# Odd layer of a fused two-block kernel: projection in 512-column half-contraction chunks, with the attention items issued between its products

## The reference, cut to what matters

```python
def odd_mixer(h, cos, sin, w_in, lam_q1, lam_k1, lam_q2, lam_k2, subln_g, w_out, lambda_init):
    b, s, _ = h.shape
    q, k, v = jnp.split(h @ w_in, 3, axis=-1)
    q = apply_rope(q.reshape(b, s, 2 * N_DIFF_HEADS, DIFF_DIM), cos, sin).reshape(b, s, N_DIFF_HEADS, 2, DIFF_DIM)
    k = apply_rope(k.reshape(b, s, 2 * N_DIFF_HEADS, DIFF_DIM), cos, sin).reshape(b, s, N_DIFF_HEADS, 2, DIFF_DIM)
    v = v.reshape(b, s, N_DIFF_HEADS, 2 * DIFF_DIM)
    lam = (jnp.exp(jnp.sum(lam_q1.astype(F32) * lam_k1.astype(F32)))
           - jnp.exp(jnp.sum(lam_q2.astype(F32) * lam_k2.astype(F32))) + lambda_init)
    o = diff_attention(q, k, v, lam)
    o = rms_norm_2(o, subln_g) * (1.0 - lambda_init)
    return o.reshape(b, s, DIFF_W) @ w_out
...
        s = jnp.einsum('bqhcd,bshcd->bhcqs', qb, k, preferred_element_type=F32) * d ** -0.5
        p = jax.nn.softmax(jnp.where(causal, s, -jnp.inf), axis=-1)
        a = p[:, :, 0] - lam * p[:, :, 1]
        return jnp.einsum('bhqs,bshe->bqhe', a.astype(v.dtype), v)
```

## Time and profile before

| | |
|---|---|
| median of 3 runs | 1993.04 us (1991.38 to 1993.1) |
| profiled execution, its own time | 1991.96 us |
| span of that profile | 1990.3 us |
| mean granted TensorE clock in the span | 0.935 of full |
| projection of the odd layer | 1256.95 to 1398.15 |
| odd layer from there to the start of `mixer_out` | 1398.15 to 1522.22 |

### The profile page before, as it was taken

How to read it: one execution, slowest core, us unless ns; L and a number is a source line. 1 busy time by engine, 2 the same in 40 slices (tenths; PEclk the granted TensorE clock), 3 DMA queues, 4 the chain that set the end, 5 groups by cost and what they waited for, 6 DMA issues and landing times.

```text
span 1990.3 us, 24899 instructions
## 1 busy us (share of the span) xinstructions
PE 1774.3 (89%) x10049; PEld 1484.2 (75%) x10049; DVE 943.5 (47%) x1232; ACT 654.2 (33%) x933; POOL 521.7 (26%) x441
## 2 busy tenths in 40 slices
PE   4997599778697789989999999899677999999997
PEld 3796499568695677668888777799566678888875
DVE  1568577675477764453333222533564343233223
ACT  4312255421223334242322212421564243333113
POOL 0005700344744000358878200078000000000000
PEclk8898799889898889999999999999878999999999
DMA  8453300134522000335556222222100212323321
GB/s 279 156 166 106 106 1 1 66 120 146 180 79 83 1 1 1 127 102 179 194 181 191 92 86 98 65 85 86 42 1 1 85 64 90 100 86 99 101 74 42
DMA packets 154445, 187.22 MB, mean 94 GB/s; under 512 B 6765, under 2 KB 121813, under 8 KB 154356
## 3 DMA queue, kind: packets, MB, share of 16 engines
q1 hardware_dynamic: 154356, 185.96, 29.0%
HBM read 183.85 MB, written 2.10 MB: 93 GB/s over the span
## 4 chain that ended last, share of the span: by engine, by line
PE 61%; POOL 15%; issue 8%; DVE 8%; ACT 5%; DMA 3%; POOLq 0%; SPq 0%; DVEq 0%; ACTq 0%
PE ps L694 7%; PE ps L695 7%; PE ps L696 7%; POOL msum L536 5%; POOL mraw L529 5%; PE ps L712 4%; PE ps L714 4%; PE ps L715 4%; PE ps L1044 4%; PE ps L1045 4%; PE ps L1046 4%; PE ps L788 2%; DMA mfirst<-in_w_mod_dram 1%; DMA mraw<-in_w_mod_dram 1%; PE ps L1017 1%
## 5 line engine op out<-in xcount | busy, mean ns | idle before, releaser
L1044 PE MATMUL ps<-uH,whi 128*128 128x512 f32 x704 | 277.6, 394 | 11.0 <-DVE uL L1581 11.0
L1565 DVE TENSOR_TENSOR wlo<-wraw,whi 128x2048 fp32r<-128x2048 f32 x71 | 176.5, 2487 | 218.8 <-ACT whi L1175 218.6
L1046 PE MATMUL ps<-uH,wlo 128*128 128x512 f32 x704 | 275.6, 392 | 0.0
L1045 PE MATMUL ps<-uL,whi 128*128 128x512 f32 x704 | 275.6, 391 | 0.0
L1175 ACT ACTIVATE whi<-wraw 128x2048 fp32r<-128x2048 f32 x71 | 135.7, 1911 | 346.8 <-PE ps L696 327.9
L712 PE MATMUL ps<-whi,uH 128*128 128x256 f32 (+1 forms) x800 | 230.8, 289 | 11.2 <-DVE uL L1581 11.2
L529 POOL TENSOR_TENSOR mraw<-mraw,cpad 128x1024 f32<-128x1024 f32 x64 | 128.4, 2007 | 398.9 <-PE ps L635 256.6
L714 PE MATMUL ps<-wlo,uH 128*128 128x256 f32 (+1 forms) x800 | 229.4, 287 | 0.0
L715 PE MATMUL ps<-whi,uL 128*128 128x256 f32 (+1 forms) x800 | 229.1, 286 | 0.0
L712 PEld LDWEIGHTS ps<-whi,uH 128*128 128x128 f32 x800 | 157.2, 196 | 12.8 <-issue 12.7
L1044 PEld LDWEIGHTS ps<-uH,whi 128*128 128x128 f32 x704 | 133.2, 189 | 41.1 <-issue 10.8
(11 more groups left out here) (389 smaller groups left out, 3200.6 us busy)
## 6 DMA issues: line engine op xcount, KB each, us to landing
mraw<-in_w_mod_dram SPq DMA_DIRECT2D x104, 512.0 KB, 3.9
wraw<-in_w_gate_dram SPq DMA_DIRECT2D x22, 1024.0 KB, 5.3
wraw<-in_w_up_dram SPq DMA_DIRECT2D x22, 1024.0 KB, 5.5
wraw<-in_w_down_dram SPq DMA_DIRECT2D x16, 1024.0 KB, 5.1
wraw<-in_w_in_odd_dram SPq DMA_DIRECT2D x12, 1024.0 KB, 5.1
wraw<-in_w_in_dram SPq DMA_DIRECT2D x11, 1024.0 KB, 5.4
wraw<-in_w_in_even_dram SPq DMA_DIRECT2D x9, 1024.0 KB, 6.5
mfirst<-in_w_mod_dram SPq DMA_DIRECT2D x16, 512.0 KB, 7.3
```

Of the source, the lines that this page charges most:

```text
L1044: mm(o, h_, uH[:, k], start=(k == 0), stop=False)
L1045: mm(o, h_, uL[:, k], start=False, stop=False)
L1046: last = mm(o, l_, uH[:, k], start=False, stop=(k == KT - 1))
L1565: V.tensor_tensor(wlo[:, n % 2, :], wraw[:, n % 2, :], whi[:, n % 2, :].bitcast(F32), ALU.subtract).then_inc(lo_done, 1)
```

## The change

The projection gets 6 pieces of 512 columns, each in two chunks of 4 contraction slices (a half), so a chunk is still 1 MB and there are still 12. The pieces are ordered by heads (`ODD_COLS`): queries and keys of heads 0 and 1; values of heads 0 to 3; queries and keys of heads 2 and 3; of 4 and 5; values of heads 4 to 7; queries and keys of heads 6 and 7. A step is three matmuls of 512 columns for one token tile and one slice, 16 steps to a half, 192 in all; a piece fills PSUM banks 0 to 3, one bank to a token tile, and the next piece uses the same banks. ACT copies tiles 0 and 2 of a piece to T1, DVE tiles 1 and 3.

PE issues 53 steps, the two jobs of head 0, 6 steps, the scores of item 0, 5 steps, and then for every item: the scores of item i + 1, the transposes of item i, a third of `STEPS[i]`, the values of item i, perhaps a job, and the rest of `STEPS[i]`. Items 0 to 18 have steps, items 19 to 31 none. ACT and DVE copy out pieces and split chunks (`odd_half_end`) at the end of the items in `HALF_END`. Scores now have one buffer, banks 4 and 5; the transposes and the jobs share bank 6; the head's output stands in bank 7. Queries and keys go to tiles of their own, `qkH` and `qkL`.

The rotary turn is made per pair of heads (`turn_pair`, 6 instructions of 256 elements for a tile): POOL turns two of the four token tiles and DVE the other two, but all four of the pair 4 and 5 are POOL's. A finished head is copied out of PSUM by DVE (`head_copy`), squared by ACT as one instruction, averaged by DVE, and scaled by POOL (`scale_head`) in two instructions of 512 elements in place of four on DVE.

The diff, cut to its core:

```diff
+ODD_COLS = ((0, 1024), (2048,), (256, 1280), (512, 1536), (2560,), (768, 1792))
+PAIR_PIECE = (0, 2, 3, 5)
+TURN_DVE = ((2, 3), (2, 3), (), (2, 3))
+STEPS = (11, 11, 10, 6, 5, 5, 6, 5, 5, 6, 5, 5, 6, 5, 5, 8, 8, 8, 8) + 13 * (0,)
+HALF_END = {1: 4, 2: 5, 5: 6, 8: 7, 11: 8, 14: 9, 16: 10, 18: 11}
+TURN_SLOT = {3: (1, 2), 4: (1, 3), 19: (3, 2), 20: (3, 3)}
+JOB_SLOT = {0: (1, 0), 1: (1, 1)}
+for _h in range(2, 8):
+    for _e in range(2):
+        JOB_SLOT[4 * _h - (4 if _h % 2 else 3) + _e] = (_h, _e)
...
                 src = sources[n]
+                if N_ODD <= n < N_ODD + 12:
+                    w = 512 // len(src)
+                    for c, part in src:
+                        sp.dma_start(wide[0][n % 2][:, :, w * c:w * c + w], part).then_inc(w_landed[n % 2], 16)
...
+            def turn_pair(r):
+                odd_out(pool, PAIR_PIECE[r], range(4))
                 for tt in range(TT):
-                    turn_heads(T1[:, tt, part * D:part * D + D], 16, (g1t, g2t)[part], tt, sem_=odd_rp, count=TT * part)
+                    if tt in TURN_DVE[r]:
+                        continue
+                    v = T1[:, tt, D + 512 * (r % 2):D + 512 * (r % 2) + 512].rearrange("p (h z f) -> p h z f", z=2, f=32)
+                    one, two = v[:, :, 0, :], v[:, :, 1, :]
+                    tm = [got[:, i, :].rearrange("p (h f) -> p h f", f=32) for i in range(4)]
+                    cs, sn = [ropet[:, i, tt:tt + 1].to_broadcast([P, 8, 32]) for i in range(2)]
+                    link(g.tensor_tensor(tm[0], one, cs, ALU.mult))
+                    link(g.tensor_tensor(tm[1], two, sn, ALU.mult))
+                    link(g.tensor_tensor(tm[2], one, sn, ALU.mult))
+                    link(g.tensor_tensor(tm[3], two, cs, ALU.mult))
...
+            def scale_head(h):
+                pool.wait_ge(ob_rd, h + 1)
+                pool.wait_ge(fac_rd, h + 1)
+                o = outb[:, h % 2, :].rearrange("p (t n) -> p t n", t=TT)
+                f = nmx[:, 4 * h:4 * h + 4].unsqueeze(2).to_broadcast([P, TT, P])
+                g.tensor_tensor(o, o, f, ALU.mult).then_inc(fo_half, 1)
+                pool.wait_ge(fo_half, h + 1)
+                g.tensor_tensor(T1[:, :, h * P:h * P + P], o, subg[:, :].unsqueeze(1).to_broadcast([P, TT, P]),
+                                ALU.mult).then_inc(fo_rd, 1)
...
+            turn_pair(0)
+            turn_pair(1)
+            scale_head(0)
+            turn_pair(2)
+            scale_head(1)
+            scale_head(2)
+            turn_pair(3)
+            for h in range(3, NH):
+                scale_head(h)
...
+            def odd_half(n):
+                p, b = divmod(n - N_ODD, 2)
                 pe.wait_ge(lo_done, n + 1)
-                acc_gone(pe, use_of(n) - 2)
-                by_token(pair[use_of(n) % 2], n, TT, uH, uL, u0=U_LN[1] if e == 0 else None).then_inc(chunk_done, 1)
-
-            def diff_job(h, e):
-                if (h, e) != (0, 1):
-                    pe.wait_ge(job_lo, 13 + 2 * h + e)
+                h_, l_ = wide[1][n % 2], wide[2][n % 2]
...
+                for s_ in range(16):
+                    tt, k = (s_ % 4, s_ // 4) if p == 0 else (s_ // 4, s_ % 4)
+                    if p == 0 and tt == 0:
+                        pe.wait_ge(u_lo, U_LN[1] + 4 * b + k + 1)
+                    if p and b == 0 and k == 0:
+                        odd_out(pe, p - 1, (tt,))
+                    o, xs, kk = acc[:, tt, :], slice(tt * P, tt * P + P), 4 * b + k
+                    mm(o, uH[:, kk, xs], h_[:, k], start=(kk == 0), stop=False)
+                    mm(o, uH[:, kk, xs], l_[:, k], start=False, stop=False)
+                    last = mm(o, uL[:, kk, xs], h_[:, k], start=False, stop=(kk == KT - 1))
+                    if kk == KT - 1 and tt < 3:
+                        last.then_inc(odd_tile, 1)
+                    if s_ == 15:
+                        last.then_inc(chunk_done, 1)
+                    yield
+
...
+            def diff_job(h, e, bank):
+                r = h // 2
+                pe.wait_ge(odd_rp, sum(TT - len(TURN_DVE[i]) for i in range(r + 1)))
+                pe.wait_ge(odd_vrp, sum(len(TURN_DVE[i]) for i in range(r + 1)))
...
                     pe.wait_ge(job_lo, 13 + 2 * h + 2)
-                if i >= 2:
-                    pe.wait_ge(fp_rd, i - 1)
+                if i >= 1:
+                    pe.wait_ge(fp_rd, i)
...
             def diff_turn(i):
                 pe.wait_ge(fa_rd, i + 1)
-                if i >= 1:
-                    pe.wait_ge(fpt_rd[(i - 1) % 2], (i - 1) // 2 + 1)
+                if i >= 1 and i - 1 in JOB_SLOT:
+                    h, e = JOB_SLOT[i - 1]
...
-                if q == 0 and h >= 2:
-                    pe.wait_ge(fo_rd, h - 1)
+                if i in (0, 16):
+                    odd_out(pe, 1 if i == 0 else 4, range(4))
+                if q == 0 and h >= 1:
+                    pe.wait_ge(ob_rd, h)
...
+                    next(halves)
+
+            more(48 + 5)
+            pe.wait_ge(mod_rd, 30)
+            diff_job(0, 0, 6)
+            diff_job(0, 1, 7)
+            more(6)
+            diff_scores(0)
+            more(5)
+            for i in range(NS):
+                if i + 1 < NS:
+                    diff_scores(i + 1)
+                diff_turn(i)
+                more(STEPS[i] // 3)
+                diff_values(i)
+                if i in JOB_SLOT:
+                    diff_job(*JOB_SLOT[i], 6)
+                more(STEPS[i] - STEPS[i] // 3)
             acc_gone(pe, use_of(N_ODD + 11))
             acc_gone(pe, use_of(N_ODD + 10))
...
-            for i in range(NS):
-                diff_turn(i)
-                if i + 2 < NS:
-                    diff_scores(i + 2)
-                if i % 4 >= 2 and i // 4 + 2 < NH:
-                    diff_job(i // 4 + 2, i % 4 - 2)
-                if i >= 1:
-                    diff_values(i - 1)
...
+            def odd_half_end(e):
                 n = N_ODD + e
-                a = use_of(n)
+                if e % 2:
+                    odd_tile_out(e // 2, 0)
+                    odd_tile_out(e // 2, 2)
                 act.wait_ge(chunk_done, n + 1)
-                A(T1[:, 0:2, WCOL * e:WCOL * e + WCOL], pair[a % 2][:, 0:512].rearrange("p (t n) -> p t n", t=2),
...
-                    act.wait_ge(lam_rd, 1)
-                    nc.scalar.preload_act_table_set(LOG_EXP)
-                    A(lam[:, 0:2], lam[:, 0:2], ACT.Exp).then_inc(lam_rd, 1)
...
+            def diff_square(h):
+                act.wait_ge(ob_rd, h + 1)
+                if h >= 1:
+                    act.wait_ge(osum_rd, h)
+                A(osq[:, :], outb[:, h % 2, :], ACT.Square).then_inc(osq_rd, 1)
...
                 ms = nmx[:, 4 * h:4 * h + 4]
-                act.wait_ge(sln_sq, 4 * h + 4)
+                act.wait_ge(sln_sq, h + 1)
                 A(ms, ms, ACT.Ln, scale=1.0 / P, bias=eps2).then_inc(sln_v, 1)
                 act.wait_ge(sln_v, h + 1)
                 A(ms, ms, ACT.Exp, scale=-0.5).then_inc(sln_rs, 1)
 
-            diff_high(0, 0)
-            diff_high(0, 1)
-            diff_high(1, 0)
+            odd_half_end(0)
+            odd_half_end(1)
+            act.wait_ge(lam_rd, 1)
+            nc.scalar.preload_act_table_set(LOG_EXP)
+            A(lam[:, 0:2], lam[:, 0:2], ACT.Exp).then_inc(lam_rd, 1)
+            odd_half_end(2)
+            diff_high(0, 0, 6)
+            diff_high(0, 1, 7)
...
             for i in range(NS):
                 diff_move(i)
-                if i + 2 < NS:
-                    diff_exps(i + 2)
...
+                if i + 1 < NS:
+                    diff_exps(i + 1)
+                if i in JOB_SLOT:
+                    diff_high(*JOB_SLOT[i], 6)
+                if i % 4 == 3:
+                    diff_square(i // 4)
+                if i in HALF_END:
+                    odd_half_end(HALF_END[i])
+                if i % 4 == 1 and i > 4:
+                    diff_root(i // 4 - 1)
+            diff_root(NH - 1)
             mixer_high(1)
             out_steps(1, N_ODD + 12)
...
+            def odd_half_end(e):
+                if e % 2:
+                    odd_tile_out(e // 2, 1)
+                    odd_tile_out(e // 2, 3)
+                split_low(N_ODD + e + 2)
...
+            def turn_pair(r, tt):
+                odd_out(dve, PAIR_PIECE[r], (tt,))
+                v = T1[:, tt, D + 512 * (r % 2):D + 512 * (r % 2) + 512].rearrange("p (h z f) -> p h z f", z=2, f=32)
...
+            def head_copy(h):
+                dve.wait_ge(fpv_rd, 4 * h + 4)
+                if h >= 2:
+                    dve.wait_ge(fo_rd, h - 1)
+                V.tensor_copy(outb[:, h % 2, :], ps[:, 7, :]).then_inc(ob_rd, 1)
+                V.reciprocal(rinv[:, 4 * h:4 * h + 4], rsum[:, 4 * h:4 * h + 4]).then_inc(dinv_rd, 1)
+
+            def head_mean(h):
+                ms = nmx[:, 4 * h:4 * h + 4]
+                dve.wait_ge(osq_rd, h + 1)
```

(44 more changed lines are left out.)

190 lines of the change are left out of this document (102 added, 88 removed).

## The result

The changed kernel took 2042.88 us (median of 4 runs, 2042.35 to 2044.81), the kernel before 1993.07 beside it: ratio 1.0252, 95% interval 1.0239 to 1.0265. The prediction was 2032 with 2008 to 2050: the side, the mechanism of the second stretch and the wide range held. The time came out 11 us above the forecast, 0.9 us outside its own range of 2020 to 2042 and 3 us from the rival *lock and clock compound* (2046).

What follows compares the result with a forecast made beforehand. PE alone was taken to bound the projection, a DVE and ACT chain of 3.5 us an item the attention. Stretches of 54.0 + 178.5 + 72.3 made 304.8 us for 265.3, so a 2032 us median; own range 2020 to 2042, wide 2008 to 2050.

Steps and rivals of the forecast that it cites:

- the mechanism of the second stretch: Items 0 to 18: at each half's end PE waits because DVE's combine is queued behind the split; idle sum 36.6 us.
- lock and clock compound: Rival: POOL's turns delay combines beside them and the last 13 items run at half clock; 14 us more, 2046 us; chance 0.13.
- First stretch: Layer start: 64 projection steps, the jobs of head 0 and the first scores; 54.0 us.
- The wait of 4 us at step 53: PE waits before the first job for DVE's turn of heads 0 and 1, which alternates with POOL's at 1.3 us; 4 us.
- Second stretch: Items 0 to 18 with 128 projection steps: products, attention work, idle waits and half clock; 178.5 us.
- hidden: Rival: the wait at a half's end is hidden and PE sets the pace; layer 246 us, 1974 us; chance 0.12.
- clock holds: Rival: the half-end waits are there but PE's clock stays up; 18 us less, 2014 us; chance 0.13.
- Third stretch: From the end of half 11 through items 19 to 31, without projection steps, to `mixer_out`; 72.3 us.
- The end of half 11: Start of the third stretch: the split for the output product delays the combine of item 19 by 5.3 us.
- a third of 50.2: One head's share of 50.2 us, the price of 12 items to the combine of item 31, turns excluded.
- 7 for the turns: DVE's two tiles of pair 3 at items 19 and 20, 2.3 us each, plus 2.4 for POOL beside the first.
- rows 10 and 11: Recorded times beside a split, read as DVE and POOL each waiting for a whole instruction of the other.

Runs made afterwards that it cites:

- combine_before_split: Changed kernel with DVE's half-end split and its copy of tile 3 moved behind the next item's combine and maxima; 1998.85 us, ratio 1.0015.
- fillers_at_half_ends: Changed kernel with 142 unread 512-column matmuls before the transposes of items 0, 3, 6, 9, 12, 15 and 17; 2028.65 us, ratio 1.0166.
- fillers: Changed kernel with unread 512-column products before the transposes' wait, 24 at item 19, 5 at each of items 20 to 31; 2034.85 us, ratio 1.0198.
- queue_reordered: Changed kernel with DVE's splits behind the combine, one DVE turn each for pairs 1 and 3, output splits at items 23 and 28; 1997.64 us, ratio 1.0001.
- wide chunks alone: Kernel before with only the projection changed, to 512-column half-contraction pieces, all ahead of the attention; 1990.81 us, ratio 0.9965.

## Why the prediction was right, and where it was off

Sum: 304.8 us predicted for the layer, 313.55 measured; the three terms were off by -5.5, +1.9 and +12.4. That the sum is off by only 8.8 us is in part luck: the first miss covers almost half of the third.

- **First stretch, 54.0 predicted, 48.47 measured.** The rate of 0.227 us a product held. The wait of 4 us at step 53 did not come, nor the 2.3 us of half clock behind it. DVE's turn and POOL's did alternate, as forecast, but a pair of instructions took 0.88 us and not 1.3, since the prediction added the two recorded times. Timeline of both:

```profile
1292.12 0.80 POOL L643 TENSOR_TENSOR T<-got 128x256 f32<-128x256 f32 x1
1292.25 0.95 DVE L2218 TENSOR_TENSOR tmp<-T,ropet 128x256 f32<-128x256 f32 x1
1293.00 0.80 POOL L644 TENSOR_TENSOR T<-got 128x256 f32<-128x256 f32 x1
1293.13 0.95 DVE L2219 TENSOR_TENSOR tmp<-T,ropet 128x256 f32<-128x256 f32 x1
...
1299.74 0.42 DVE L2221 TENSOR_TENSOR T<-tmp 128x256 f32<-128x256 f32 x1
```

Alone the DVE instruction takes 0.42 us, as taken; beside POOL it takes 0.95 and POOL's 0.80 instead of 0.72. DVE's 12 took 9.7 us where 12 pairs of 1.3 are 15.6, and the job began at 1300.31 with the tiles just ready.

- **Second stretch, 178.5 predicted, 180.35 measured.** Idle before the transposes 36.75 us against 36.6, half clock 34.3 us long and so 17.2 lost against 16.1. The longest wait, 6.85 us before item 15 against 5.1, is the one whose combine POOL's scaling meets (2.93 us for 0.97), which the prediction had not counted; the wait before item 4 was 0.9 for 1.5. Shown by undoing them: without idle time and half clock 52 us less up to item 19 (`combine_before_split`), with the idle time but without the clock 13 less (`fillers_at_half_ends`), of which some 3 may be the scatter named above. The rivals *hidden* and *clock holds* fall: in the changed kernel the seven waits and the half clock behind each are in the trace, and each went only with one of these edits.

- **Third stretch, 72.3 predicted, 84.73 measured: the mis-sized term.** The end of half 11 was right (5.0 to combine 19, 5.3 predicted). The rest, by heads: 19 to 23 took 28.2 us against 23.7 (a third of 50.2, and 7 for the turns), 23 to 27 took 22.7 and 27 to 31 17.1 against 16.7 each, the tail 11.7 against 9.8. The prediction said of the scores "at half clock" and of the rest nothing. From combine 19 to `mixer_out` the clock was 0.54, and fillers, which lift it to 0.90, take 4.8 us off the 12 items and 2.0 off the tail, which becomes 9.7 where 9.8 was predicted. At a clock of 1.00 the heads 23 to 27 and 27 to 31 are 19.6 and 16.4 us. The second thing not priced is POOL's scaling beside a combine. The prediction moved the scaling to POOL and counted it in the tail alone, though it had the rule from rows 10 and 11. The four combines at the ends of the heads (items 19, 23, 27 and 31) are 1.0, 2.0, 0.7 and 0.7 us longer for POOL. What is left is as priced: the 50.2 us hold four jobs of 1.15, so a head without jobs is a third of 45.6, 15.2 us, and one with two jobs 17.5; at full clock and less POOL's part they took 15.8 and 17.6. The jobs themselves took 0.9 us each for 1.15, and the turns were right as well (4.7 and 2.25 us on DVE, 6.9 for the 7). That the head 27 to 31 came to 17.1 beside a third of 50.2 is luck: that third holds the price of jobs which this head has not. The rival *lock and clock compound* named both causes, at 14 us; it had POOL's turns where the trace has mostly its scaling. The clock part is shown by the fillers. POOL's part is read from the timelines; no run moved the scaling.

- **Where the expected gain went.** The covering of items 0 to 18 works once the queue is in order: 181.5 us to item 19 for 216.0, a gain of 34.5, of which 7 are the wide chunks. But the 13 items that have no products left take 81.6 us to `mixer_out` for 49.2 (`queue_reordered`), 32.4 given back: one score buffer, the head copy and the turns now stand in the chain, at a clock of 0.61, with POOL beside four combines. Which of these costs how much is shown for the clock alone (4.1 us net by the fillers); no run gave the second score buffer back. The two cancel. The order of DVE's queue explains 46 of the 48 us that the changed kernel lost; it does not bring a gain over wide chunks alone.
